# Feed-forward up projections from seven block products per pair of column tiles, and the first tap of their convolution on ScalarE

## Chip, cores, metric

The kernel runs on one core of a Trainium2 chip. The metric is the device time of one execution in microseconds (us); lower is better. TensorE is called PE here, VectorE DVE, ScalarE ACT, and SP is the engine that issues most of the DMAs.

## The reference, cut to what matters

The program is one transformer-like block with attention, a delta rule and a mixture of experts, followed by two layers (an attention mixer and an SSM mixer), each with a feed-forward. All is float32, with 512 tokens (T) and width 1024 (D). The change touches only the two feed-forwards:

```
D_FF = 2816
FFN_K = 3
...
def conv_ffn(xn, w_up, conv_w, conv_b, w_down):
    h = causal_dwconv(xn @ w_up, conv_w, conv_b)
    return (jax.nn.silu(h[..., :D_FF]) * h[..., D_FF:]) @ w_down
```

`xn @ w_up` has 2 x 2816 columns. The depthwise convolution runs along the tokens with three taps and a bias. The first 2816 columns are the gate, the others the value.

## The kernel before

Work is laid out transposed: features on the 128 partitions, tokens along the free dimension. `hT` holds the normalised input, 8 chunks (DC) of 128 features by 512 tokens. The 2816 columns are FC = 22 tiles of 128, so there are 22 pairs of a gate tile and a value tile. Weights arrive in a ring of RING = 4 slots of 1 MB, which SP refills in order: a slot is loaded again when PE has begun on the next slot (`slot_free`). One slot holds what one pair needs, 8 blocks of 128x128 for the gate tile and 8 for the value tile.

For each pair PE makes 16 matmuls of 128x512, in two accumulations of 8 (`dense`, one for each half of the pair), into two PSUM banks that alternate (`bank()`, `tile_free`, `tile_done`). ACT copies each bank to `fpad`, a buffer with two zero columns ahead of the 512 tokens. DVE does the three taps of each half: the first with the bias as one tensor_scalar (L2522), the other two as scalar_tensor_tensor (L2526). ACT then does the Silu of the gate half (L2497), and DVE multiplies both halves into `ff` (L2534). `fpad`, `fy` and `fgate` are single buffers, so the convolution of one pair ends before that of the next begins. Two pairs are written out, and the other 20 run in a hardware loop of four pairs. A small memset (L2542, `ff_ready`) then lets PE start the down projections, 22 matmuls for each of 8 output tiles; they read all of `ff`.

Each engine has one queue, written by hand, in program order. All matmuls are issued from one helper line, L391. One float32 matmul leaves two weight-load records and two matmul records in the trace, so a pair's 16 matmuls are 32 records. ffn_a is the first feed-forward and ffn_b the second; the same functions write both.

Of the kernel before, what the change touches and what calls it, by code (L numbers as in the profile page):

```python
# [405 lines left out]
def blocks(slot, first, n, width=P):  # L406
    return [slot[:, P * (first + k):P * (first + k) + width] for k in range(n)]


def program(nc, x, p, stream, vecs, consts, ssm, out):  # L410
    with ExitStack() as ctx:
# [28 lines left out]
        def V(name):  # L440
            lo, hi = VEC[name]
            return vec[:, lo:hi]
# [2010 lines left out]
        ff = a(FC, T)  # L2453
        fpad, fy = a(2, 2 + T), a(2, T)
        fgate = a(T)
        fw, fb = a(2, 3), a(2, 1)
        FF_HEAD = FC % 4

        def ffn_pe(e, before_last=None):
            def up(first=False):  # L2460
                e.eng.wait_ge(S[e.landing()], e.landed())
                w = e.slot(ring)
                for half in range(2):
                    e.eng.wait_ge(S["tile_free"], e.c["tile"].at(-1))
                    e.dense(e.bank(), blocks(w, 8 * half, 8), [hT[:, k, :] for k in range(DC)],
                            h_ready if first and half == 0 else None)
            for s in range(FF_HEAD):
                up(s == 0)
            with loop(e, FC // 4, fill=4, tile=8):
                for s in range(4):  # L2470
                    up()
            e.eng.wait_ge(S["ff_ready"], e.c["ff_ready"].next())
            for m in range(DC):
                if m == DC - 1 and before_last is not None:
                    before_last(e)
                e.eng.wait_ge(S["tile_free"], e.c["tile"].at(-1))
                o = e.bank()
                for part in range(2):
                    e.eng.wait_ge(S[e.landing()], e.landed())
                    w = e.slot(ring)  # L2480
                    for k in range(FC // 2):
                        kk = part * (FC // 2) + k
                        ins = e.mm(o, w[:, P * k:P * k + P], ff[:, kk, :], kk == 0, kk == FC - 1)
                ins.then_inc(S["tile_done"], 1)
            norm_sum_pe(e)

        def ffn_act(e, before_down=None, before_last=None):
            def up():
                e.eng.wait_ge(S["pads_free"], e.c["pads_free"].next())
                for half in range(2):  # L2490
                    e.eng.wait_ge(S["tile_done"], e.c["tile"].next())
                    t = e.result()
                    e.eng.wait_ge(S["tile_free"], e.c["tile"].at(-1))
                    nc.scalar.activation(fpad[:, half, 2:2 + T], t, ACT.Copy).then_inc(S["tile_free"], 1)  # L2494
                    e.eng.wait_ge(S["tile_free"], e.c["tile"].at())
                e.eng.wait_ge(S["gate_ready"], e.c["gate_ready"].next())
                nc.scalar.activation(fgate, fy[:, 0, :], ACT.Silu).then_inc(S["gate_silu"], 1)  # L2497
            for s in range(FF_HEAD):
                up()
            with loop(e, FC // 4, tile=8, pads_free=4, gate_ready=4):  # L2500
                for s in range(4):
                    up()
            if before_down is not None:
                before_down(e)
            residual_act(e, before_last)

        def ffn_dve(e, gain, wname, bname, meanwhile=None):
            normalize_dve(e, gain)
            fwv = V(wname).rearrange("p (j n) -> p j n", n=6)
            fbv = V(bname).rearrange("p (j n) -> p j n", n=2)  # L2510
            nc.vector.memset(fpad[:, :, 0:2], 0.0).then_inc(S["dve_chain"], 1)
            e.eng.wait_ge(S["dve_chain"], e.c["dve_chain"].next())

            def up(j):
                nc.vector.tensor_copy(fw.rearrange("p a b -> p (a b)"), dyn(fwv, j)).then_inc(S["dve_chain"], 1)
                e.eng.wait_ge(S["dve_chain"], e.c["dve_chain"].next())
                nc.vector.tensor_copy(fb.rearrange("p a b -> p (a b)"), dyn(fbv, j)).then_inc(S["pads_free"], 1)
                e.eng.wait_ge(S["pads_free"], e.c["pads_free"].next())
                for half in range(2):
                    e.eng.wait_ge(S["tile_free"], e.c["tile"].next())  # L2520
                    y = fy[:, half, :]
                    nc.vector.tensor_scalar(y, fpad[:, half, 2:2 + T], fw[:, half, 2:3], fb[:, half, :],  # L2522
                                            ALU.mult, ALU.add).then_inc(S["dve_chain"], 1)
                    e.eng.wait_ge(S["dve_chain"], e.c["dve_chain"].next())
                    for t in range(2):
                        ins = nc.vector.scalar_tensor_tensor(out=y, in0=fpad[:, half, t:t + T], scalar=fw[:, half, t:t + 1],  # L2526
                                                             in1=y, op0=ALU.mult, op1=ALU.add)
                        if (half, t) != (0, 1):
                            ins.then_inc(S["dve_chain"], 1)
                            e.eng.wait_ge(S["dve_chain"], e.c["dve_chain"].next())  # L2530
                    if half == 0:
                        ins.then_inc(S["gate_ready"], 1)
                e.eng.wait_ge(S["gate_silu"], e.c["gate_silu"].next())
                nc.vector.tensor_tensor(dyn(ff, j), fgate, fy[:, 1, :], ALU.mult).then_inc(S["dve_chain"], 1)  # L2534
                e.eng.wait_ge(S["dve_chain"], e.c["dve_chain"].next())

            for s in range(FF_HEAD):
                up(s)
            with loop(e, FC // 4, tile=8, pads_free=4, gate_silu=4, dve_chain=28) as i:
                for s in range(4):  # L2540
                    up(i * 4 + (FF_HEAD + s))
# [530 lines left out]
        @block.scalar  # L3072
        def _(act):
            e = start(Engine, "act", act)
            load_act(e)
            e.skip(2 * NB)
            e.eng.wait_ge(S["stage"], e.c["stage"].next())
            e.mark("values")
            values_act(e)
            e.eng.wait_ge(S["stage"], e.c["stage"].next())  # L3080
            e.mark("attn")
            attn_act(e)
            e.eng.wait_ge(S["stage"], e.c["stage"].next())
# [24 lines left out]
            nc.scalar.activation(dt_, V("s_dt"), ACT.Exp).then_inc(S["ssm_scalars"], 1)  # L3108
            ffn_act(e, ssm_scalars_act, ssm_turn_act)
# [5 lines left out]
            ffn_act(e)  # L3115
            e.eng.wait_ge(S["stage"], e.c["stage"].next())
            e.mark("out")
            final_act(e)

        @block.vector  # L3120
        def _(dve):
# [36 lines left out]
            ffn_dve(e, "ffn0", "f0_w", "f0_b", ssm_tables_dve)  # L3158
# [5 lines left out]
            ffn_dve(e, "ffn1", "f1_w", "f1_b")  # L3164
# [34 lines left out]
```

## Time and profile before

| | |
|---|---|
| median of 3 runs | 2922.38 us (2921.68 to 2924.26) |
| profiled execution, its own time | 2924.33 us |
| its span, first to last instruction | 2922.5 us |
| PE busy in the span | 2830.5 us (97%) |
| DVE busy | 1076.7 us (37%) |
| ACT busy | 550.9 us (19%) |
| mean granted clock of PE | 0.976 of full speed |

The span is what the trace covers. Busy time is the time in which an engine had at least one instruction under way; issuing, branches and waits are not counted.

### The profile page before, as it was taken

To read this page: it belongs to the slowest core of one execution; us is meant where nothing else is said; L and a number is where in the kernel's file an instruction comes from. 1 tells how busy PE (TensorE), PEld (TensorE's weight loads), DVE (VectorE), ACT (ScalarE), POOL (GpSimd) and SP (SyncE) were. 2 spreads that over 40 slices of the span, in tenths; PEclk is the share of its full clock that TensorE was granted. 3 is DMA by queue.
4 is the path that set the end of the run, shared out by engine and by line. 5 is a ranking of instruction groups with operands and counts; after the bars stand their busy time and mean duration, and the time that the engine had idled before them with its cause. 6 is when DMAs were issued, how large, how long until landed. Compare 5 with 4: busy or idle time off the path is not lost.

```text
span 2922.5 us, 26887 instructions
## 1 busy us (share of the span) xinstructions
PE 2830.5 (97%) x10294; PEld 1471.7 (50%) x10294; DVE 1076.7 (37%) x2357; ACT 550.9 (19%) x991; POOL 0.2 (0%) x4
## 2 busy tenths in 40 slices
PE   8999999999999999999999989999999999999998
PEld 4544446676674446444444455444444664444444
DVE  1244445556542012000033864333345663333201
ACT  2154532212301002010011143111110121111101
POOL 0000000000000000000000000000000000000000
PEclk9999989999999997999999989999999999999999
DMA  4111111101012220444412201222222211222232
GB/s 177 58 58 48 54 44 44 44 29 44 29 44 86 87 76 29 163 170 169 166 60 100 72 15 44 79 72 74 84 86 103 86 53 64 73 85 72 75 112 101
DMA packets 32936, 228.56 MB, mean 78 GB/s; under 512 B 3520, under 2 KB 4160, under 8 KB 6080
## 3 DMA queue, kind: packets, MB, share of 16 engines
q1 hardware_dynamic: 31440, 223.70, 21.5%
q10 hardware_dynamic: 1392, 3.41, 0.3%
q8 instruction: 74, 1.21, 0.2%
q14 instruction: 30, 0.25, 0.0%
HBM read 224.99 MB, written 2.10 MB: 78 GB/s over the span
## 4 chain that ended last, share of the span: by engine, by line
PE 93%; DVE 4%; ACT 2%; issue 1%; DMA 0%; DVEq 0%; ACTq 0%
PE psum L391 91%; DVE work L2316 1%; PE psum L769 1%; DVE hT L550 0%; PE psum L1078 0%; DVE work L696 0%; PE psum L2180 0%; PE psum L1879 0%; PE psum L1691 0%; PE psum L2999 0%; DVE xT L1622 0%; DMA mixT<-x_dram 0%; ACT work L521 0%; ACT work L589 0%; PE psum L612 0%
## 5 line engine op out<-in xcount | busy, mean ns | idle before, releaser
L391 PE MATMUL psum<-hT,ring 128*128 128x512 f32 (+1 forms) x3920 | 1325.0, 517 | 13.5 <-ACT work L1207 5.4
L391 PEld LDWEIGHTS psum<-hT,ring 128*128 128x128 f32 (+1 forms) x3920 | 575.6, 172 | 659.5 <-issue 645.2
L391 PE MATMUL psum<-work,ring 128*128 128x512 f32 (+1 forms) x1040 | 453.4, 597 | 16.7 <-DVE ticks L2542 8.0
L391 PEld LDWEIGHTS psum<-work,ring 128*128 128x128 f32 x1040 | 199.4, 193 | 267.0 <-issue 244.1
L391 PE MATMUL psum<-work 128*128 128x128 f32 (+7 forms) x2258 | 297.5, 286 | 14.2 <-ACT work L2278 10.9
L391 PEld LDWEIGHTS psum<-work 128*128 128x128 f32 (+2 forms) x2258 | 251.7, 178 | 109.3 <-issue 72.3
L391 PE MATMUL psum<-ring,work 128*128 (+1 forms) x568 | 248.9, 597 | 1.4 <-ACT mixT L1747 0.8
L2522 DVE TENSOR_SCALAR work<-work 128x512 f32<-128x512 f32 x88 | 48.0, 546 | 352.3 <-ACT work L2494 352.3
L391 PEld LDWEIGHTS psum<-ring,work 128*128 128x128 f32 x568 | 107.6, 192 | 132.8 <-issue 129.2
L2494 ACT ACTIVATE work<-psum 128x512 f32<-128x512 f32 x88 | 52.6, 597 | 529.4 <-PE psum L391 512.2
L391 PE MATMUL psum<-ring,hT 128*128 128x512 f32 (+2 forms) x368 | 147.6, 558 | 3.2 <-DVE work L696 1.1
L391 PE MATMUL psum<-mixT,ring 128*128 128x512 f32 x320 | 142.6, 599 | 0.7 <-ACT work L1203 0.7
L2526 DVE SCALAR_TENSOR_TENSOR work<-work 128x512 f32<-128x512 f32 x176 | 132.3, 752 | 6.2
L1622 DVE TENSOR_TENSOR xT<-xT,psum 128x512 f32<-128x512 f32 x40 | 27.5, 687 | 257.3 <-PE psum L391 257.3
L391 PEld LDWEIGHTS psum<-ring,hT 128*128 128x128 f32 x368 | 86.7, 256 | 59.6 <-issue 39.6
L521 ACT ACTIVATE work<-xT 128x512 f32<-128x512 f32 x56 | 35.2, 628 | 393.8 <-DVE xT L1622 393.1
L391 PEld LDWEIGHTS psum<-mixT,ring 128*128 128x128 f32 x320 | 61.1, 193 | 73.5 <-issue 70.9
L2316 DVE SCALAR_TENSOR_TENSOR work<-work,vec 128x512 f32<-128x512 f32 x112 | 84.1, 751 | 3.6
L1972 DVE SCALAR_TENSOR_TENSOR work<-psum,work 128x256 f32<-128x256 f32 x28 | 13.2, 483 | 188.8 <-ACT work L1954 188.3
L391 PE MATMUL psum<-work,con 128*32 128x127 f32 (+4 forms) x288 | 80.4, 463 | 2.2 <-ACT work L1349 1.1
L391 PE MATMUL psum<-con,work 128*128 128x64 f32 (+6 forms) x576 | 72.6, 253 | 8.7 <-DVE work L529 5.4
L391 PEld LDWEIGHTS psum<-con,work 128*128 128x128 f32 (+2 forms) x576 | 67.0, 175 | 15.3 <-DVE work L529 7.1
(369 smaller groups left out, 1647.6 us busy)
## 6 DMA issues: line engine op xcount, KB each, us to landing
ring<-stream_dram SPq DMA_DIRECT2D x208, 1024.0 KB, 4.8
con<-consts_dram SPq DMA_DIRECT2D x1, 2953.0 KB, 13.5
mixT<-x_dram ACTq DMA_DIRECT2D x4, 512.0 KB, 6.6
out_dram<-work SPq DMA_DIRECT2D x2, 1024.0 KB, 4.2
work<-p_dram ACTq DMA_DIRECT2D x1, 512.0 KB, 3.7
con<-ssm_dram ACTq DMA_DIRECT2D x1, 512.0 KB, 3.2
vec<-vecs_dram SPq DMA_DIRECT2D x1, 378.0 KB, 6.0
work<-consts_dram ACTq DMA_DIRECT2D x1, 256.0 KB, 2.6
```

The source lines that it names most:

```text
L391: ins = self.eng.matmul(out, lhsT, rhs, start=start, stop=stop)
L521: nc.scalar.activation(squares[:, k, :], xT[:, k, :], ACT.Square).then_inc(S["x_squares"], 1)
L769: ins = e.eng.transpose(psum[:, 2, at:at + P], a_pr[:, u.d, at:at + P], ident)
L1622: nc.vector.tensor_tensor(xT[:, m, :], xT[:, m, :], e.result(), ALU.add).then_inc(S["tile_free"], 1)
L1972: nc.vector.scalar_tensor_tensor(out=act_tok[:, s, :], in0=psum[:, gate_up_bank(ex, s), 256:512], scalar=slot_weight[:, ex, s:s + 1], in1= ...
L2316: ins = nc.vector.scalar_tensor_tensor(out=y, in0=upad[:, j, t:t + T], scalar=taps_w[:, j, t:t + 1], in1=y, op0=ALU.mult, op1=ALU.add)
L2494: nc.scalar.activation(fpad[:, half, 2:2 + T], t, ACT.Copy).then_inc(S["tile_free"], 1)
L2522: nc.vector.tensor_scalar(y, fpad[:, half, 2:2 + T], fw[:, half, 2:3], fb[:, half, :], ALU.mult, ALU.add).then_inc(S["dve_chain"], 1)
L2526: ins = nc.vector.scalar_tensor_tensor(out=y, in0=fpad[:, half, t:t + T], scalar=fw[:, half, t:t + 1], in1=y, op0=ALU.mult, op1=ALU.add)
```

## The change

The first pair is computed as before. For the 21 others (FAST) the product of weights and `hT` is cut into 2x2 blocks: rows into gate and value tile, the 1024 features into two halves of 4 chunks, and the columns into the early and the late 256 tokens. Instead of the 8 block products, 7 are made, of sums and differences of blocks (the Winograd form of Strassen's scheme). A product is 4 matmuls of 128x256, and each goes into a PSUM bank of its own (`seven`, all eight banks in turn). What comes with it:

- DVE makes four sums of `hT` blocks once for each feed-forward (`h_sums`, 128x1024 each) and four sums of weight blocks for each pair (`weight_sum`, 128x512 each, in two sets of buffers `w_sums`), reading the ring slot one pair ahead of PE.
- ACT copies product 0 out of PSUM (`base`, 128x256); DVE makes the seven additions that turn products into the four quarters of `fpad` (`read`, 128x256 each, numbered 0 to 6; `seven_read` counts them).
- ACT does the first tap and the bias (`tap0`) from `fpad` with activation Identity, where DVE's tensor_scalar was; DVE no longer copies taps and bias to small buffers. DVE keeps four taps per pair (`tap`).
- The loops over four pairs are gone; all pairs are written out. In DVE's queue the convolution of one pair (`tap`, `gated`) is mixed with the reads of the next pair and the weight sums of the pair after.

```diff
+            for j in range(FAST):
                 e.eng.wait_ge(S[e.landing()], e.landed())
                 w = e.slot(ring)
...
+                def product(i, weights, moving):
+                    for k in range(4):
+                        ins = e.mm(seven(j, i), weights[k], moving[k], k == 0, k == 3)
+                    ins.then_inc(S["seven"], 1)
+
+                if j >= 2:
+                    e.eng.wait_ge(S["seven_read"], 7 * (n + j - 1))
+                product(0, a11, b11)
+                e.eng.wait_ge(S["w_sum"], 4 * (n + j) + 3)
...
+                    e.eng.wait_ge(S["base_in"], n + j)
+                product(1, s2, t2)
...
+                product(2, s1, t1)
...
+                product(3, s3, t3)
...
+                product(4, a12, b21)
+                e.eng.wait_ge(S["w_sum"], 4 * (n + j) + 4)
...
+                product(5, s4, b22)
...
+                product(6, a22, t4)
...
+            for j in range(FC):
+                if j < FAST:
+                    e.eng.wait_ge(S["seven"], 7 * (n + j) + 1)
...
+                    nc.scalar.activation(base[:, j % 2, :], seven(j, 0), ACT.Copy).then_inc(S["base_in"], 1)
+                if j > 0:
+                    e.eng.wait_ge(S["seven_read"], 7 * (n + j))
                 for half in range(2):
...
+                    nc.scalar.activation(fy[:, half, :], fpad[:, half, 2:2 + T], ACT.Identity, scale=V(wname)[:, at:at + 1],
+                                         bias=V(bname)[:, 2 * j + half:2 * j + half + 1]).then_inc(S["tap0"], 1)
+                e.eng.wait_ge(S["gate_ready"], m + j + 1)
                 nc.scalar.activation(fgate, fy[:, 0, :], ACT.Silu).then_inc(S["gate_silu"], 1)
...
+                    read(fast, 5)
+                    read(fast, 6)
+                    e.eng.wait_ge(S["seven_read"], 7 * (n + j))
+                if j + 1 < FAST:
+                    weight_sum(j + 1, 0)
+                for t in (1, 2):
+                    for half in range(2):
+                        tap(j, half, t)
+                        if after and (half, t) == (1, 1):
+                            read(j, 0)
+                if after:
+                    e.eng.wait_ge(S["tap"], e.c["tap"].at(3))
+                    read(j, 1)
+                    read(j, 2)
+                    read(j, 3)
+                if j + 1 < FAST:
+                    weight_sum(j + 1, 2)
+                    weight_sum(j + 1, 1)
+                gated(j)
+                if j + 1 < FAST:
+                    weight_sum(j + 1, 3)
+                if after:
+                    read(j, 4)
```

PE's queue, from the second pair of ffn_a on. Before, in the loop, one pair is two rows of 8 matmuls:

```order
L2461 REGISTER_ALU
L2464 REGISTER_ALU
L391 MATMUL psum<-hT,ring 128x512 x8
L2464 REGISTER_ALU
L391 MATMUL psum<-hT,ring 128x512 x8
```

In the changed kernel one pair is these five rows (product 0; products 1 to 3, whose weights are sums in `mixT` and whose moving operands are sums in `work`; product 4; 5; 6):

```order
L391 MATMUL psum<-hT,ring 128x256 x4
L391 MATMUL psum<-work,mixT 128x256 x12
L391 MATMUL psum<-hT,ring 128x256 x4
L391 MATMUL psum<-hT,mixT 128x256 x4
L391 MATMUL psum<-work,ring 128x256 x4
```

So 16 matmuls of 512 columns became 28 of 256 columns, and the sums that 20 of them need come from DVE.

DVE's queue for the gate half of a pair in the loop before (copies of taps and bias, then three taps; the value half has three more, and L2534 multiplies the two):

```order
L2515 COPY work<-vec 128x6
L2516 ISA
L2517 ISA
L2517 COPY work<-vec 128x2
L2518 REGISTER_ALU
L2520 ISA
L2522 TENSOR_SCALAR work<-work 128x512
L2524 REGISTER_ALU
L2526 SCALAR_TENSOR_TENSOR work<-work 128x512
L2530 REGISTER_ALU
L2526 SCALAR_TENSOR_TENSOR work<-work 128x512
```

DVE's queue for one pair in the changed kernel, from the weight sum after read 6 to reads 4, 5 and 6 (L2589 are weight sums, L2614 taps, L2603 reads, L2621 the product with the gate):

```order
L2589 TENSOR_TENSOR mixT<-ring 128x512
L2614 SCALAR_TENSOR_TENSOR work<-work,vec 128x512 x2
L2603 TENSOR_TENSOR work<-work,psum 128x256
L2614 SCALAR_TENSOR_TENSOR work<-work,vec 128x512 x2
L2603 TENSOR_TENSOR work<-work,psum 128x256 x3
L2589 TENSOR_TENSOR mixT<-ring 128x512
L2589 TENSOR_TENSOR mixT<-mixT,ring 128x512
L2621 TENSOR_TENSOR work<-work 128x512
L2589 TENSOR_TENSOR mixT<-ring,mixT 128x512
L2603 TENSOR_TENSOR work<-work,psum 128x256 x3
```

Seven large operations per pair (and two small copies) became sixteen large ones: four weight sums, four taps, one product, seven reads.

## Rows read from the trace of the kernel before

**Rows 1.** The page: busy time by engine; the chain that ended last, by engine
```profile
PE 2830.5 (97%) x10294; PEld 1471.7 (50%) x10294; DVE 1076.7 (37%) x2357; ACT 550.9 (19%) x991; POOL 0.2 (0%) x4
...
PE 93%; DVE 4%; ACT 2%; issue 1%; DMA 0%; DVEq 0%; ACTq 0%
```

**Rows 2.** Windows, both up stages: us, busy by engine, PE clock, DMA share, GB/s
```profile
1853.00:2152.00 299.00, 299.00 (x698) 132.69 (x697) 109.81 (x192) 40.19 (x65) 0.00 (x0) 1.00 0.22 76
2455.00:2747.00 292.00, 292.00 (x682) 129.33 (x680) 107.80 (x190) 39.60 (x64) 0.00 (x0) 1.00 0.21 75
```

**Rows 3.** What PE waited for, 1853 to 2157 us: total, times, longest
```profile
PE psum L391 <- DVE ticks L2542: 4.0, 1, 4.0
```

**Rows 4.** Timeline of PE, runs of 512 and 128 columns: start, length, records
```profile
600.49 3.73 PE L391 MATMUL psum<-work 128*128 128x128 f32 x32
604.06 2.31 PE L391 MATMUL psum<-hT,ring 128*128 128x512 f32 x5
...
2559.56 80.85 PE L391 MATMUL psum<-hT,ring 128*128 128x512 f32 x188
```

**Rows 5.** Timeline of PE, runs of 256 columns, in the mixer
```profile
1692.25 1.13 PE L391 MATMUL psum<-work,ring 128*128 128x256 f32 x4 [0.42 <-ACT hT L2237]
...
1707.95 0.60 PE L391 MATMUL psum<-work,hT 96*128 96x256 f32 x2
1708.39 1.19 PE L391 MATMUL psum<-work 128*128 128x512 f32 x4
```

**Rows 6.** Groups by shape, PE: busy, mean ns | idle before, releasers
```profile
L391 PEld LDWEIGHTS psum<-hT,ring 128*128 128x128 f32 x2880 | 543.8, 192 | 649.4 <-issue 635.2 <-DVE ticks L366 3.7 <-PE psum L391 3.6
L391 PE MATMUL psum<-work 128*128 128x256 f32 x72 | 19.0, 382 | 0.5 <-DVE work L904 0.5
```

**Rows 7.** Groups by shape, DVE
```profile
L2526 DVE SCALAR_TENSOR_TENSOR work<-work 128x512 f32<-128x512 f32 x176 | 132.3, 752 | 6.2
L1495 DVE TENSOR_TENSOR work<-work,psum 128x512 f32<-128x512 f32 x40 | 27.6, 691 | 18.4 <-PE psum L391 18.4
L2680 DVE TENSOR_TENSOR con<-con 128x256 f32<-128x256 f32 x18 | 7.7, 427 | 0.6
```

**Rows 8.** Timeline of DVE: L2587 needs no result of L2586, L2590 needs both
```profile
2292.99 0.69 DVE L2586 TENSOR_TENSOR mixT<-mixT,con 128x512 f32<-128x512 f32 x1
2293.59 0.69 DVE L2587 TENSOR_TENSOR mixT<-mixT,con 128x512 f32<-128x512 f32 x1
2294.31 0.69 DVE L2590 TENSOR_TENSOR mixT<-mixT 128x512 f32<-128x512 f32 x1
```

**Rows 9.** Groups by shape, ACT
```profile
L2497 ACT ACTIVATE work<-work 128x512 f32<-128x512 f32 x44 | 27.7, 630 | 1.4
L1954 ACT ACTIVATE work<-psum 128x256 f32<-128x256 f32 x28 | 10.3, 382 | 165.5 <-PE psum L391 164.0 <-DVE work L1972 1.4
L2295 ACT ACTIVATE mixT<-work,vec 128x512 f32<-128x512 f32 x4 | 2.6, 710 | 0.0
```

**Rows 10.** Timeline of all engines, from the last up matmul of ffn_a on
```profile
2152.72 0.60 ACT L2494 ACTIVATE work<-psum 128x512 f32<-128x512 f32 x1 [6.27 <-PE psum L391]
...
2155.62 0.69 DVE L2534 TENSOR_TENSOR work<-work 128x512 f32 x1
2156.55 0.06 DVE L2542 MEMSET ticks<- 128x1 f32 x1 [0.24 <-DVE work L2534]
...
2156.66 23.74 PE L391 MATMUL psum<-work,ring 128*128 128x512 f32 x51 [3.98 <-DVE ticks L2542]
```

**Rows 11.** Timeline at the start of ffn_a
```profile
1848.96 31.63 PE L391 MATMUL psum<-hT,ring 128*128 128x512 f32 x69
...
1852.39 0.06 DVE L2511 MEMSET work<- 128x4 f32 x1
```

**Rows 12.** Windows, written-out code of the SSM mixer; what SP's queue waited for
```profile
2300.00:2350.00 50.00, 46.96 (x945) 38.18 (x947) 37.58 (x56) 7.96 (x14) 0.00 (x0) 0.93 0.17 54
...
SPq L3178 <- PE psum L391: 2753.6, 204, 77.0
```

More of the change, by code:

```diff
@@ new lines, in ffn_pe @@
+        def ffn_pe(e, before_last=None):
+            e.eng.wait_ge(S[e.landing()], e.landed())
+            w = e.slot(ring)
+            for half in range(2):
+                e.eng.wait_ge(S["tile_free"], e.c["tile"].at(-1))
+                e.dense(e.bank(), blocks(w, 8 * half, 8), [hT[:, k, :] for k in range(DC)], h_ready if half == 0 else None)
+            n = e.c["fast"].n
+            fill_at[n] = e.c["fill"].n
+            early, late = slice(0, HALF), slice(HALF, T)
+            for j in range(FAST):
@@ L2461, in up @@
                 e.eng.wait_ge(S[e.landing()], e.landed())
                 w = e.slot(ring)
[L2463 to L2471, printed above, removed]
+                ws = w_sums[:, j % 2, :, :]
@@ L2505, in ffn_act, with ffn_dve @@
             residual_act(e, before_last)
-        def ffn_dve(e, gain, wname, bname, meanwhile=None):
+        def ffn_dve(e, gain, wname, meanwhile=None):
             normalize_dve(e, gain)
[L2509 to L2515, printed above, removed]
-                e.eng.wait_ge(S["dve_chain"], e.c["dve_chain"].next())
[L2517 to L2541, printed above, removed]
@@ new lines, in ffn_dve @@
+            n = e.c["fast"].n
+            nc.vector.memset(fpad[:, :, 0:2], 0.0).then_inc(S["pads_free"], 1)
+            e.eng.wait_ge(S["pads_free"], e.c["pads_free"].next())
+            e.eng.wait_ge(S["h_ready"], e.c["h_ready"].at())
+            k1, k2, early, late = slice(0, 4), slice(4, 8), slice(0, HALF), slice(HALF, T)
+            for i, (o, in0, in1) in enumerate(((0, hT[:, k1, late], hT[:, k1, early]), (2, hT[:, k2, late], hT[:, k1, late]),
+                                               (1, hT[:, k2, late], h_sums[:, 0, :, :]),
+                                               (3, hT[:, k2, early], h_sums[:, 1, :, :]))):
+                if i >= 2:
+                    e.eng.wait_ge(S["h_sum"], 4 * (n // FAST) + (1, 3)[i - 2])
+                nc.vector.tensor_tensor(h_sums[:, o, :, :], in0, in1, ALU.subtract).then_inc(S["h_sum"], 1)
@@ new lines, in weight_sum @@
+            def weight_sum(j, i):
+                f = fill_at[n] + j
+                w = ring[:, f % RING, :]
+                a11, a12, a21, a22 = (w[:, 512 * q:512 * q + 512] for q in range(4))
+                ws = w_sums[:, j % 2, :, :]
+                if i == 0:
+                    e.eng.wait_ge(S["loaded%d" % (f % RING)], 16 * (f // RING + 1))
+                if j >= 2:
+                    e.eng.wait_ge(S["seven"], 7 * (n + j - 2) + 6)
+                o, in0, in1, op = ((0, a21, a22, ALU.add), (1, ws[:, 0, :], a11, ALU.subtract),
+                                   (2, a11, a21, ALU.subtract), (3, a12, ws[:, 1, :], ALU.subtract))[i]
+                if i in (1, 3):
+                    e.eng.wait_ge(S["w_sum"], 4 * (n + j) + i)
+                nc.vector.tensor_tensor(ws[:, o, :], in0, in1, op).then_inc(S["w_sum"], 1)
@@ new lines, in read @@
+            def read(j, i):
+                b = base[:, j % 2, :]
+                o, in0, product, own = ((with_low, b, 1, None), (with_add, with_low, 2, 1), (fpad[:, 1, 2 + HALF:2 + T], with_add, 3, 2),
+                                        (with_low, with_low, 3, 2), (fpad[:, 0, 2:2 + HALF], b, 4, None),
+                                        (fpad[:, 0, 2 + HALF:2 + T], with_add, 5, 3), (fpad[:, 1, 2:2 + HALF], with_low, 6, 4))[i]
+                in1 = seven(j, product)
+                e.eng.wait_ge(S["seven"], 7 * (n + j) + product + 1)
+                if i == 0:
+                    e.eng.wait_ge(S["base_in"], n + j + 1)
+                    e.eng.wait_ge(S["seven_read"], 7 * (n + j))
+                if own is not None:
+                    e.eng.wait_ge(S["seven_read"], 7 * (n + j) + own)
+                nc.vector.tensor_tensor(o, in0, in1, ALU.add).then_inc(S["seven_read"], 1)
@@ new lines, in tap @@
+            def tap(j, half, t):
+                y = fy[:, half, :]
+                at = 6 * j + 3 * half
+                wv = V(wname)[:, at:at + 3]
+                done = S["gate_ready"] if (half, t) == (0, 2) else S["tap"]
+                if t == 1:
+                    e.eng.wait_ge(S["tap0"], e.c["tap0"].next())
+                else:
+                    e.eng.wait_ge(S["tap"], e.c["tap"].at(half + 1))
+                nc.vector.scalar_tensor_tensor(out=y, in0=fpad[:, half, t - 1:t - 1 + T], scalar=wv[:, t - 1:t],
+                                               in1=y, op0=ALU.mult, op1=ALU.add).then_inc(done, 1)
@@ L2542, in ffn_dve @@
+            e.c["fast"].n += FAST
             nc.vector.memset(e.ticks, 0.0).then_inc(S["ff_ready"], 1)
```

82 lines of the change are left out of this document (61 added, 21 removed).

## The prediction

> **What bounds the kernel now.** I read the page first: PE is busy for 97% of the span and is 93% of the chain that ended last [rows 1]. Then the windows of the two up stages: PE is busy for all of the 299 and 292 us, at a granted clock of 1.00, which is the 2.4 GHz level, while DVE is busy 110 of 299 us and ACT 40 [rows 2]. Then the waits of PE over ffn_a's up stage: one, 4.0 us, at its end, for the memset behind DVE's last product [rows 3]. So the up stage is a plain stream of matmul records, and it moves with the number of records and the pace of one; the other engines cost only at its two ends.
>
> The pace is read from long runs in the timeline. 188 records of 512 columns take 80.85 us, which is 0.429 us each (the last one's length of 0.6 taken off) [rows 4]. A pair has 32 records: 13.73 us. Records of 128 columns, each with a weight load of its own, start 32 to 3.57 us (600.49 to 604.06), 0.1116 us each [rows 4].
>
> **PE, pair by pair.** A changed pair has 28 matmuls, 56 records of 256 columns. No long run of that form is in the trace, so the pace comes from both sides. On the line through the two runs it is 0.1116 + 128 x (0.429 - 0.1116)/384 = 0.2174 us. The lower end is half a 512 record, 0.2145. Two records of 256 columns in the mixer start the next work 0.44 us after the first of them, 0.22 each [rows 5]; a group of four takes 1.13 us, which is 3 x 0.2174 + 0.38, the length of one such record, and 0.10 over for the first weight load, which nothing hides after the engine has been idle [rows 5, 6]. I take 0.2174, since the line already contains a weight load and a share of waits. A pair is then 56 x 0.2174 = 12.17 us, 1.56 less than 13.73. 21 pairs in each of two feed-forwards: 42 x 1.56 = 65.4 us less. With 0.2145 it would be 72.2 less, with 0.22 59.2.
>
> The point at which nothing is gained is 13.73/56 = 0.245 us per record.
>
> Against this change speaks a rule of the Trainium skill. Rows first: a 128-column load is recorded at 192 ns in the up stage [rows 6], while 128-column matmuls with their loads follow each other every 0.1116 us [rows 4], so loads lie beside matmuls that use all rows of the array. "TensorE: Matmul & The Clock Gate", section on packing small matmuls, says that a weight load overlaps a matmul in flight only when they use different row groups. By that rule half as many columns per load would double the exposed loads. The rows above do not bear it out; what it would cost is among the rivals.
>
> **DVE, whether it keeps up.** Per pair it gets four weight sums and the product with the gate, at 0.691 each, four taps at 0.752, and seven reads at 0.427 (SBUF operands; with 512 columns a PSUM operand costs the same as none, 691 to 690) [rows 7, 8]. That is 3.46 + 3.01 + 2.99 = 9.45 us. Operations that do not need the one ahead start 0.60 apart, those that do 0.72, for a length of 0.69 [rows 8], so the queue takes between 9.45 - 16 x 0.09 = 8.0 and 9.45 + 16 x 0.03 = 9.9 us. Both are under 12.17. Before, it was 0.37 of a pair (5.0 us) [rows 2]; this engine goes from slack to about three quarters full.
>
> Order and waits matter more than the sum. Set the end of product 6 of the pair before to 0; products end every 1.74 us, at 1.7, 3.5, 5.2, 7.0, 8.7, 10.4, 12.2. DVE: read 6 to 0.5; a weight sum to 1.2. ACT stands behind product 0 (its copy comes first in its queue), copies at 1.75 to 2.15 (0.382), then does two Identity operations of 0.63 to 0.71 (Silu's length and that of an operation with a scale from `vec`) [rows 9], so the first DVE tap starts near 2.9. Two taps, read 0 (needs product 1, 3.5), two taps, read 1: to about 6.5. Reads 2 and 3 wait for product 3 at 7.0 and end at 7.8. Two weight sums to 9.0, the product with the gate (Silu ended near 6) to 9.8, the last weight sum to 10.4, reads 4 and 5 to 11.2, then a wait for product 6 at 12.2. DVE ends each round some 1.0 us early.
>
> What PE waits for in its turn: product 1 of the next pair needs the third weight sum. It is ready at 9.0 and wanted at 12.2 + 1.7 = 13.9, 4.9 us of cover. If it were gone, PE would stand in every pair. The bank waits (reads 0 to 5 of the pair before) are a whole pair old. Product 0 needs the reads of the pair before last. So the ring of waits costs nothing as long as a DVE round is under 12.17 us. Per pair ACT has 0.38 + 2 x 0.71 + 0.63 = 2.4 us, no bound.
>
> **The two ends.** At the end PE stood 3.98 us before: copy, first tap, two taps, product, memset [rows 10]. Now: read 6 (0.43), ACT's first tap (0.63 to 0.71), three DVE taps started 0.65 apart and the fourth, Silu of the gate half beside it, the product 0.69, and the same 0.35 from its end to PE (2155.62 + 0.69 to 2156.66) [rows 7, 9, 10]. The taps start at 1.2; the gate's second ends at 1.2 + 1.3 + 0.75 = 3.25, Silu at 3.95, the product at 4.7, PE at 5.05. That is 1.1 us later, twice: +2.1 us. At the start the four `hT` sums (twice the length of a 512-column operation at most, 1.38) and the first four weight sums are 8.3 us on DVE from 1852.4, so to 1860.8 [rows 7, 11]; the first pair keeps PE until at least 1848.96 + 13.73 = 1862.7 [rows 11], and product 0 for 1.7 more. Cost nothing; without that cover it would be 8.3 us per feed-forward.
>
> **Edits at nothing.** The code is written out instead of looped, over 9 PE instructions per us; the SSM mixer's written-out part runs 945 matmuls and 947 loads in 50 us, 38 per us [rows 12]. Its supply can hold this. Ring: a slot is used every 12.2 instead of 13.7 us, SP waits for PE 2753.6 us in all, not for DMA, and the DMA share of the stage is 0.22 [rows 2, 12]. DVE's small copies and first tap lay under PE before; their removal gives nothing by itself.
>
> **Sum.** -65.4 + 2.1 = -63.3 us. The profiled execution had 2924.33 us, 1.8 above its span; it becomes 2861.0. It lies 1.95 above the median of the runs shown, so the median becomes 2859.1. With the low pace: 2922.4 - 72.2 + 2 = 2852; with 0.22: 2865.
>
> **Rivals.**
> 1. *Each product pays for its wait.* All seven products start behind a wait of their own. For: after idle time the first load costs 0.10 us [rows 5]. Against: the loop before had waits and register work every 16 records and kept 0.429, and loads lie beside matmuls there. If all seven paid it: 7 x 0.10 x 42 = 29 us, time 2888. A third of it gives 2869.
> 2. *The weight load is not hidden under 256 columns* (slower). Its place is every record of the 42 pairs. For: nothing in the trace is a long run of 256 columns, and records of 512 hide a load of 192 ns easily, records of 256 only just. Against: the 0.1116 of 128 columns and the 0.22 of 256 [rows 4, 5]. If each record paid the 0.10 of a first load, a pair is 56 x 0.317 = 17.75 us, +4.02 x 42 = +169, with the ends 3093. It decides from 0.245 us per record, 0.028 above mine.
>  By the row-group rule of the Trainium skill (same page and section), with the page's own load time of columns/1.2 ns, an estimate is 0.107 us more per record, much the same in time, and a quarter of this rival's chance is its; the trace disagrees.
> 3. *DVE becomes the bound.* For: sixteen large operations and a queue in fixed order. Against: 9.9 us at the most by rows. It would need 0.15 us more at each of the sixteen to reach PE's 12.17, and 0.24 to reach 13.73, from where it is slower. At a round of 13.0 it is 42 x 0.73 less, 2894; at 15 it is 42 x 1.27 more, 2978.
>
> **How the numbers follow.** The main case has 0.80, with 2850 to 2868 as its own range (paces 0.2145 to 0.22, the ends, and a part of the waits). Rival 1 in the rest of its reach, 2868 to 2890, has 0.11. Rival 2 has 0.04, rival 3 0.04 (half of it above 2922), and 0.01 goes to no change. The range 2848 to 2880 holds the main case and most of rival 1. About 0.2%, 6 us, is what a measurement of this kernel can tell: faster 0.93, same 0.01, slower 0.06.
>
> **What would show it.** The window of an up stage with PE busy all through at clock 1.00 and 0.217 us per record; an up stage of 13.7 + 21 x 12.2 = 269 us instead of 302; DVE busy about 75% there, each round ending in a wait for PE; the wait for the memset at 5.0 us. Wrong would be: waits of PE for DVE's weight sums or reads inside the stage, idle "issue" in PE between products, a granted clock under 1.00, table loads on ACT between Identity and Silu, or DVE operations well longer than those of rows 7.

## The result

| | before | changed |
|---|---|---|
| median | 2923.32 us (2921.68 to 2924.57, 4 runs) | 2852.48 us (2851.28 to 2859.27, 4 runs) |
| ratio of the runs | | 0.9769 (0.9756 to 0.9782) |
| profiled execution, its span | 2922.5 us | 2849.5 us |

The change is faster by 2.3%. A second set, 4 runs of the changed kernel beside 25 further runs of the kernel before (median 2918.60 us), gave 0.9770 (0.9753 to 0.9788). All ratios below are to such runs of the kernel before, taken beside the kernel in question; each has its 95% interval behind it. The predicted 2859 us is a ratio of 0.978.

The page of the changed kernel, busy time by engine:

```profile
PE 2753.9 (97%) x11302; PEld 1658.9 (58%) x11302; DVE 1226.2 (43%) x2651; ACT 578.4 (20%) x1037; POOL 0.2 (0%) x4
```

PE lost 77 us of busy time and is still busy for 97% of a shorter span [rows 1]. DVE gained 150 us; of these only what stands at the two ends of the stages shows in the time, 1.1 us each, as the rows below tell.

Windows inside the two up stages of the changed kernel (us, busy by engine, PE clock, DMA share, GB/s):

```profile
1860.00:2105.00 245.00, 245.00 (x1137) 215.68 (x1136) 172.59 (x325) 48.41 (x81) 0.00 (x0) 1.00 0.25 86
2430.00:2670.00 240.00, 240.00 (x1113) 211.28 (x1112) 168.69 (x317) 48.35 (x80) 0.00 (x0) 1.00 0.26 88
```

PE is busy all the time at the full clock, as before [rows 2], and DVE for 70% in place of 37%. What PE waited for in the whole program, the row of the memset behind the last product (L2656 is L2542 of before):

```profile
PE psum L391 <- DVE ticks L2656: 10.3, 2, 5.1
```

5.1 us twice, where it was 4.0 [rows 3]. Between the first and the last product of a stage the timeline of PE shows no wait at all.

One round in the timeline of the changed kernel, PE, DVE and ACT together:

```profile
1962.63 1.89 PE L391 MATMUL psum<-hT,ring 128*128 128x256 f32 x8
1962.83 0.42 DVE L2603 TENSOR_TENSOR work<-work,psum 128x256 f32<-128x256 f32 x1 [1.24 <-PE psum L391]
1963.28 0.69 DVE L2589 TENSOR_TENSOR mixT<-ring 128x512 f32<-128x512 f32 x1
...
1964.36 5.34 PE L391 MATMUL psum<-work,mixT 128*128 128x256 f32 x24
1964.56 0.38 ACT L2547 ACTIVATE work<-psum 128x256 f32<-128x256 f32 x1 [7.86 <-PE psum L391]
1964.84 1.51 ACT L2552 ACTIVATE work<-work,vec 128x512 f32<-128x512 f32 x2
1965.67 1.46 DVE L2614 SCALAR_TENSOR_TENSOR work<-work,vec 128x512 f32<-128x512 f32 x2 [1.70 <-ACT work L2552]
...
1968.82 0.42 DVE L2603 TENSOR_TENSOR work<-work,psum 128x256 f32<-128x256 f32 x1
1969.54 1.89 PE L391 MATMUL psum<-hT,ring 128*128 128x256 f32 x8
1969.73 0.75 DVE L2603 TENSOR_TENSOR work<-work,psum 128x256 f32<-128x256 f32 x2 [0.50 <-PE psum L391]
...
1974.92 0.42 DVE L2603 TENSOR_TENSOR work<-work,psum 128x256 f32<-128x256 f32 x1 [1.24 <-PE psum L391]
...
1976.44 5.34 PE L391 MATMUL psum<-work,mixT 128*128 128x256 f32 x24
```

The reader is to see two things. The row of products 1 to 3 starts again after 12.08 us (1964.36 to 1976.44), and PE's rows carry no idle time in brackets. Over ten rounds it is 12.09 us (1855.58 to 1976.44), 0.2158 us for each of 56 records. And DVE, from read 6 to read 6 (1962.83 to 1974.92), stands three times: 1.70 us for ACT's first tap, 0.50 for product 3, 1.24 for product 6. That is 3.44 us in 12.09, so DVE's own work is 8.65.

The end of ffn_a's up stage, which answers to [rows 10]:

```profile
2107.87 0.42 DVE L2603 TENSOR_TENSOR work<-work,psum 128x256 f32<-128x256 f32 x1 [1.31 <-PE psum L391]
2108.32 1.52 ACT L2552 ACTIVATE work<-work,vec 128x512 f32<-128x512 f32 x2 [6.56 <-DVE work L2603]
2109.24 2.74 DVE L2614 SCALAR_TENSOR_TENSOR work<-work,vec 128x512 f32<-128x512 f32 x4 [0.95 <-ACT work L2552]
2111.35 0.63 ACT L2555 ACTIVATE work<-work 128x512 f32<-128x512 f32 x1 [1.51 <-DVE work L2614]
...
2112.08 0.69 DVE L2621 TENSOR_TENSOR work<-work 128x512 f32<-128x512 f32 x1
...
2112.84 0.06 DVE L2656 MEMSET ticks<- 128x1 f32 x1
...
2112.96 67.53 PE L391 MATMUL psum<-work,ring 128*128 128x512 f32 x150 [5.13 <-DVE ticks L2656]
```

Read 6, two first taps on ACT, four taps on DVE, Silu, the product, the memset: a chain with PE standing.

### The profile page after: what moved, and what is told of

Its sections match the earlier page's. It is cut to its first block, busy times and chain, and to the rows that moved or that the text cites. A ratio compares the mean times of both kernels' runs of the same rounds, so it can differ in the third digit from the quotient of the medians.

```text
span 2849.5 us, 28832 instructions
## 1 busy us (share of the span) xinstructions
PE 2753.9 (97%) x11302; PEld 1658.9 (58%) x11302; DVE 1226.2 (43%) x2651; ACT 578.4 (20%) x1037; POOL 0.2 (0%) x4
## 4 chain that ended last, share of the span: by engine, by line
PE 93%; DVE 4%; ACT 2%; issue 1%; DMA 0%; DVEq 0%; ACTq 0%
PE psum L391 91%; DVE work L2316 1%; PE psum L769 1%; DVE hT L550 0%; PE psum L1078 0%; DVE work L696 0%; PE psum L2180 0%; PE psum L1879 0%; PE psum L3113 0%; DVE xT L1622 0%; ACT work L521 0%; ACT work L589 0%; DVE work L2614 0%; DMA mixT<-x_dram 0%; ACT mixT L1729 0%
## 5 line engine op out<-in xcount | busy, mean ns | idle before, releaser
L391 PE MATMUL psum<-hT,ring 128*128 128x512 f32 (+2 forms) x3248 | 905.2, 458 | 13.8 <-ACT work L1207 5.5
L391 PEld LDWEIGHTS psum<-hT,ring 128*128 128x128 f32 (+1 forms) x3248 | 447.2, 168 | 355.1 <-issue 323.8
L391 PE MATMUL psum<-work,ring 128*128 128x512 f32 (+1 forms) x1376 | 532.5, 543 | 18.9 <-DVE ticks L2656 10.3
L391 PEld LDWEIGHTS psum<-work,ring 128*128 128x128 f32 x1376 | 262.8, 192 | 277.3 <-issue 244.3
L391 PE MATMUL psum<-work,mixT 128*128 128x256 f32 (+2 forms) x1200 | 258.6, 379 | 2.0 <-ACT work L1732 1.5
L391 PEld LDWEIGHTS psum<-work,mixT 128*128 128x128 f32 (+1 forms) x1200 | 207.1, 181 | 44.7 <-issue 16.1
L2614 DVE SCALAR_TENSOR_TENSOR work<-work,vec 128x512 f32<-128x512 f32 x176 | 125.6, 748 | 74.4 <-ACT work L2552 74.4
L2603 DVE TENSOR_TENSOR work<-work,psum 128x256 f32<-128x256 f32 x294 | 115.8, 417 | 77.5 <-PE psum L391 76.1
L2316 DVE SCALAR_TENSOR_TENSOR work<-work,vec 128x512 f32<-128x512 f32 x112 | 84.1, 751 | 3.6
L2547 ACT ACTIVATE work<-psum 128x256 f32<-128x256 f32 x42 | 16.1, 384 | 316.5 <-PE psum L391 316.5
```

The costliest lines, as they stand in the source:

```text
L391: ins = self.eng.matmul(out, lhsT, rhs, start=start, stop=stop)
L2316: ins = nc.vector.scalar_tensor_tensor(out=y, in0=upad[:, j, t:t + T], scalar=taps_w[:, j, t:t + 1], in1=y, op0=ALU.mult, op1=ALU.add)
L2547: nc.scalar.activation(base[:, j % 2, :], seven(j, 0), ACT.Copy).then_inc(S["base_in"], 1)
L2603: nc.vector.tensor_tensor(o, in0, in1, ALU.add).then_inc(S["seven_read"], 1)
L2614: nc.vector.scalar_tensor_tensor(out=y, in0=fpad[:, half, t - 1:t - 1 + T], scalar=wv[:, t - 1:t], in1=y, op0=ALU.mult, op1=ALU.add).then_ ...
```

## Experiments

**Two more traces.** Both kernels were run again unchanged, because the two first traces differ by 73 us while the predicted sum was 63: some 10 us lay ahead of ffn_a, in code that the change does not touch.

> The kernel before, unchanged, for a second trace of it. In the two traces so far the part of the program ahead of ffn_a, which the change does not touch, ends 10.2 us apart: the first hT operation of ffn_a (L550) starts at 1847.1 us before and at 1836.9 us after. Theory 1 (those 10 us are chance of the clock dips and no part of the change): over the runs this start moves by several us either way, in this kernel too. Theory 2 (the longer written-out code shifts something in the unchanged part for good): it is again 1847 within 2 us here, and 1837 in every kernel with the written-out code. Time 2923 by both.

> The changed kernel, unchanged, for a second trace and a second ratio. Theory 1: L550 of ffn_a starts anywhere from 1837 to 1848, the part behind it takes 1012.6 us again, the median lies between 2851 and 2860. Theory 2: 1837 within 2 us again, and a median of 2852.

Measured: 2919.44 us (ratio 0.9997, 0.9985 to 1.0009) and 2854.21 us (0.9770, 0.9753 to 0.9788). The first `hT` operation of ffn_a stands at 1847.1 us in the first trace of before (5.3 us ahead of the memset in [rows 11]). In the timeline of the changed kernel:

```profile
1836.89 5.36 DVE L550 SCALAR_TENSOR_TENSOR hT<-xT,vec,psum 128x512 f32<-128x512 f32 x8 [1.83 <-PE psum L391]
```

In the second trace of before:

```profile
1840.07 5.35 DVE L550 SCALAR_TENSOR_TENSOR hT<-xT,vec,psum 128x512 f32<-128x512 f32 x8 [2.17 <-PE psum L391]
```

And in the second of the changed kernel:

```profile
1840.79 5.36 DVE L550 SCALAR_TENSOR_TENSOR hT<-xT,vec,psum 128x512 f32<-128x512 f32 x8 [1.81 <-PE psum L391]
```

The looped kernel was 7 us earlier in its second trace, the written-out one 4 us later. Over all traces of this study the start lies at 1840.1 to 1847.1 in the five looped kernels and at 1836.9 to 1843.3 in the seven written out. The idea that it stays at 1847 in the one and at 1837 in the other falls. What moves it is not shown. What is behind that point took 1075.4 and 1078.3 us before (span less start), and 1012.6 and 1012.6 after: 63 to 66 us less.

That stretch still holds code that the change does not touch: the down projections, the SSM mixer and the program's end. To take them out, the two up stages are measured alone, each up to the first down matmul. PE's rows at the start of ffn_b's up stage and of its down projections, before:

```profile
2443.22 304.05 PE L391 MATMUL psum<-hT,ring 128*128 128x512 f32 x704 [0.93 <-DVE hT L550]
2751.25 109.22 PE L391 MATMUL psum<-work,ring 128*128 128x512 f32 x247 [3.98 <-DVE ticks L2542]
```

And in the changed kernel:

```profile
2403.24 18.53 PE L391 MATMUL psum<-hT,ring 128*128 128x512 f32 x40 [0.93 <-DVE hT L550]
2678.99 121.49 PE L391 MATMUL psum<-work,ring 128*128 128x512 f32 x279 [5.12 <-DVE ticks L2656]
```

ffn_b, from its first up matmul to its first down matmul, takes 308.0 us before and 275.8 after. ffn_a, from its first `hT` operation to its first down matmul, takes 309.6 (1847.1 to 2156.66 [rows 10]) and 276.1 (1836.89 to 2112.96). Both stages together are 617.6 and 618.1 us in the two traces of before, and 551.8 in both of the changed kernel: 65.8 to 66.3 us less. The stretch between the two stages, from the first down matmul of ffn_a to the first up matmul of ffn_b, is unchanged code; it took 286.6 and 289.6 before and 290.3 and 290.3 after.

**The form of the records alone.**

```diff
-                    e.dense(e.bank(), blocks(w, 8 * half, 8), [hT[:, k, :] for k in range(DC)],
...
+                    o = e.bank()
...
+                    for cols in (slice(0, T // 2), slice(T // 2, T)):
+                        for k in range(DC):
+                            ins = e.mm(o[:, cols], blocks(w, 8 * half, 8)[k], hT[:, k, cols], k == 0, k == DC - 1)
+                    ins.then_inc(S["tile_done"], 1)
```

The first pair of each stage stays as it was, and so does the loop over four pairs.

> The kernel before with each 128x512 matmul of 21 pairs (all but the first two pairs' first) of the up stage cut into two of 128x256 into the same bank: 64 records of 256 columns per pair in place of 32 of 512, all 8 block products, no sums. Theory 1 (pace of a record is its columns and 2.5 ns, weight loads hidden): 64 x 0.2158 = 13.81 us per pair in place of 13.73, +0.08 x 42 = +3.5 us, 2927. Rival (the pace of 0.2158 depends on few loads per stretch or on the sums' short groups, a load shows under longer runs): more than 13.9 us per pair, over 2930. The difference to the changed kernel, which keeps the form of the records and drops one product in eight, is then what the seventh of the products is worth: 8 x 0.2158 x 42 = 72.5 us.

Measured: 2923.44 us, ratio 1.0009 (0.9998 to 1.0021). Its timeline in the up stage, PE:

```profile
1869.66 90.60 PE L391 MATMUL psum<-hT,ring 128*128 128x256 f32 x419
```

(90.60 - 0.38)/418 = 0.2158 us, the same as in the changed kernel, with twice as many weight loads per column as before. Its two up stages, measured as above, take 621.4 us against 617.6 and 618.1, so 3.3 to 3.8 more where 3.5 were expected. All that the cut into 256 columns costs is the fixed part of a record; the gain is the product that is left out. This kernel has the loop and the changed one has not, and both run at 0.2158, so writing the pairs out gave PE nothing either.

**The first tap on ACT alone**, in the kernel before:

```diff
+                    nc.scalar.activation(fy[:, half, :], fpad[:, half, 2:2 + T], ACT.Identity, scale=fw[:, half, 2:3],
+                                         bias=fb[:, half, :]).then_inc(S["tap0"], 1)
...
-                    nc.vector.tensor_scalar(y, fpad[:, half, 2:2 + T], fw[:, half, 2:3], fb[:, half, :],
-                                            ALU.mult, ALU.add).then_inc(S["dve_chain"], 1)
-                    e.eng.wait_ge(S["dve_chain"], e.c["dve_chain"].next())
+                    e.eng.wait_ge(S["tap0"], e.c["tap0"].next())
```

> The kernel before with only the second part of the change: the first tap and bias of each half done by ACT behind its copy, in place of DVE's operation; the taps still come from the small copies. Theory 1 (PE sets the up stage, this lies under it): no change in the stage, and at each of the two ends 0.80 us (ACT's length in the changed kernel) in place of 0.55, so +0.5 us: 2923 to 2924. Rival (moving it off DVE was itself a gain): under 2918.

Measured: 2920.30 us beside 2918.60 of before, ratio 1.0000 (0.9989 to 1.0012), where +0.5 us or nothing was expected; the interval is 3 us to each side. PE's waits at the two ends went from 8.0 to 8.5 us in all, as expected.

**The first tap back on DVE**, in the changed kernel:

```diff
-                    nc.scalar.activation(fy[:, half, :], fpad[:, half, 2:2 + T], ACT.Identity, scale=V(wname)[:, at:at + 1],
-                                         bias=V(bname)[:, 2 * j + half:2 * j + half + 1]).then_inc(S["tap0"], 1)
...
+                    nc.vector.tensor_scalar(fy[:, half, :], fpad[:, half, 2:2 + T], V(wname)[:, at:at + 1],
+                                            V(bname)[:, 2 * j + half:2 * j + half + 1], ALU.mult, ALU.add).then_inc(S["tap0"], 1)
```

> The changed kernel with the first tap and its bias back on DVE (one tensor_scalar of 0.55 us for each half, ahead of the other taps); everything else stays. Theory 1 (PE sets the stage as long as DVE's round is under 12.09 us): DVE has 3.4 us of waits per round and gets 1.1 more work, of which the wait for ACT's tap (1.7 us) goes away, so the stage stays at 12.09 per pair. At the ends DVE's first tap stands in place of ACT's 0.80, but both halves lie on DVE: +0.3 us each. Within 1 us of the changed kernel, 2852 to 2856. Rival (the two parts of the change need each other, DVE would become the bound): 42 x 0.5 us or more, over 2873.

Measured: 2854.58 us, ratio 0.9771 (0.9756 to 0.9786); the changed kernel's 0.9769 and 0.9770 lie within that interval. PE's wait at each end is 5.2 us. The window of its up stage:

```profile
1870.00:2105.00 235.00, 235.00 (x1091) 206.87 (x1090) 183.50 (x350) 20.04 (x40) 0.00 (x0) 1.00 0.26 90
```

DVE is busy for 78% and PE still for all of it. The second half of the change is worth nothing that these runs can tell, with the seven products or without them, where a difference under some 4 us would not show.

**How much room DVE has.** Three, six and nine more additions of 128x512 per pair:

```diff
+                for s in range(9):
+                    if s >= 2:
+                        e.eng.wait_ge(S["spare"], e.c["spare"].at(-1))
+                    nc.vector.tensor_tensor(spare[:, s % 2, :], xT[:, 0, :], xT[:, 1, :], ALU.add).then_inc(S["spare"], 1)
+                    e.c["spare"].n += 1
                 gated(j)
```

> The changed kernel with nine more DVE additions of 128x512 per pair into a spare buffer, between the weight sums and the product with the gate. They are extra work and change no result. Each takes 0.60 us of DVE's queue. Theory 1 (DVE's round is 8.65 us of work and 3.4 us of waits that all can give way): 8.65 + 5.4 = 14.1 us, a little more for ACT's first tap, so 2.0 to 2.3 us over PE's 12.09 for 42 pairs and 5.4 at each end: +95 to +107 us, 2950 to 2962. Rival (waits in fixed order do not give way, each addition costs its full time): 5.4 x 44 = +238 us, 3092. Rival (DVE has more room than that): under 2920.

> The changed kernel with three more DVE additions of 128x512 per pair into a spare buffer, at the same place as the nine. Theory 1: 1.8 us more in a round with 3.4 us of waits; the stage stays at 12.09 us per pair. The wait before read 6 (1.24) goes and read 6 comes 0.6 us later; the wait for ACT's tap takes that up. Only at the end of each stage it shows, 1.8 us behind the taps, of which Silu (0.7) covers a part, and 0.6 ahead of them: +3 to +5 us in all, 2856 to 2859. Rival (every addition to DVE shows, as the nine did with 5.4 us of work against 2.2 us of time per pair): +26 us or more.

> The same with six more. Theory 1: the round with nine measured 14.25 us, three fewer are 1.8 less, 12.45, just over PE's 12.09: 0.3 to 0.4 us per pair, +13 to +17 in the stages and 3 to 7 at the ends, 2869 to 2878. This is the threshold: with fewer, DVE's work is free, from here on each costs its 0.60. Rival as for three: +100 us.

| additions | time | ratio (95%) | DVE's round | PE's round | PE's wait at each end |
|---|---|---|---|---|---|
| 0 (two sets) | 2852.48, 2854.21 us | 0.9769, 0.9770 | 12.09 us | 12.09 us | 5.1 us |
| 3 | 2854.41 us | 0.9777 (0.9760 to 0.9795) | 12.09 us | 12.09 us | 6.7 us |
| 6 | 2876.11 us | 0.9847 (0.9830 to 0.9863) | 12.44 us | 12.09, then 12.44 us | 14.0 us |
| 9 (2 runs) | 2955.06 us | 1.0116 (1.0096 to 1.0137) | 14.25 us | 12.09, then 14.25 us | 19.2 us |

The timeline of the kernel with nine, one round:

```profile
1967.85 0.69 DVE L2590 TENSOR_TENSOR mixT<-mixT,ring 128x512 f32<-128x512 f32 x1
1968.45 5.50 DVE L2654 TENSOR_TENSOR work<-xT 128x512 f32<-128x512 f32 x9
1968.59 5.45 PE L391 MATMUL psum<-work,mixT 128*128 128x256 f32 x24 [1.66 <-DVE mixT L2590]
1973.87 0.68 DVE L2622 TENSOR_TENSOR work<-work 128x512 f32<-128x512 f32 x1
...
1982.70 5.50 DVE L2654 TENSOR_TENSOR work<-xT 128x512 f32<-128x512 f32 x9
```

Here DVE is the bound, and PE stands 1.66 us of each round for the third weight sum, the wait that the prediction named as the first to fail. The other 0.5 us of the 2.16 that a round got longer lie in PE's rows beside its waits; products 1 to 3, for one, take 5.45 us behind the stand where they took 5.34. 1.8 us of DVE's work left the round at 12.09, 5.4 made it 2.16 longer, and from six to nine each addition costs 0.60 us of the round. With nine the kernel is slower than before.

The table has a second reading. With six, DVE's round is 12.44 us from the start, but PE does not follow it until late. PE's row of products 1 to 3 in that kernel:

```profile
2015.51 5.34 PE L391 MATMUL psum<-work,mixT 128*128 128x256 f32 x24
...
2027.59 5.34 PE L391 MATMUL psum<-work,mixT 128*128 128x256 f32 x24
...
2039.92 5.45 PE L391 MATMUL psum<-work,mixT 128*128 128x256 f32 x24
...
2052.36 5.45 PE L391 MATMUL psum<-work,mixT 128*128 128x256 f32 x24
```

For 14 rounds, from 1858.38 to 2027.59, PE keeps 12.09 us; then it takes 12.33 and 12.44. That is what the cover of 4.9 us for the third weight sum, worked out in the prediction, allows: DVE falls back 0.35 us per round, and 14 x 0.35 is 4.9. With nine the cover lasts three rounds. What DVE has fallen back by is paid at the end of the stage, where PE waits for DVE's last product, and with it the additions of the last pair: 4.9 + 6 x 0.60 = 8.5 us would be this estimate for six, and the wait grew by 8.9. For nine it would be 10.3 and the wait grew by 14.1, so not all of that is accounted for. From the first up matmul of ffn_a to the last, PE took 270.0 us in the changed kernel and 272.2 with six additions; the wait behind it went from 5.1 to 14.0. So of the 22 us that six additions cost in the two stages, 18 are at the ends and only 4 in the rounds. With nine the ends have 28 us of 101. The expectations for six and nine put 3 to 7 and 11 us there and more into the rounds; that their times came out (2869 to 2878 and 2950 to 2962 us) is in part two errors that cancel. With three the time was a little under the 2856 to 2859 expected; the two waits at the ends grew by 3.2 us in all, within its 3 to 5.

**Down projections that don't wait for the last tile.** PE stands 5.1 us twice for the last of 22 tiles, which it reads only in its 22nd matmul.

```diff
-            e.eng.wait_ge(S["ff_ready"], e.c["ff_ready"].next())
+            e.eng.wait_ge(S["ff_part"], e.c["ff_part"].next())
...
                         kk = part * (FC // 2) + k
+                        if m == 0 and kk == FC - 1:
+                            e.eng.wait_ge(S["ff_ready"], e.c["ff_ready"].next())
...
                 gated(j)
+                if j == FC - 2:
+                    nc.vector.memset(e.ticks, 0.0).then_inc(S["ff_part"], 1)
```

In the kernel before, the same is done with a small memset behind the product of every pair, so it has 22 memsets more per feed-forward.

> The changed kernel, but PE may begin the down projections when 21 of the 22 tiles of ff are there (a memset behind the product of tile 20 lets it), and waits for the last tile only ahead of the 22nd matmul of the first output tile, some 18 us of matmuls later. Theory 1 (the 5.1 us stand at each end is the whole cost of the tail, and the records behind it run slow for a few us): the two waits of 5.1 us go, and with them part of the slow records, 10 to 17 us less: 2836 to 2844 at a level of 2853. Rival (the time of the tail comes back as a wait at the 22nd matmul or at the next bank): less than 3 us.

> The kernel before with the same early start of the down projections (a small memset per pair counts the tiles of ff). Theory 1: its two waits of 4.0 us go, 8 us and part of the slow records behind them, 8 to 14 us less, so a ratio of 0.995 to 0.997. It is then the fair partner for the changed kernel with the early start: the difference of the two is 42 x 1.64 = 69 us, without the 2.3 us of longer tails. Rival as above: ratio 0.999 or more.

Measured: 2837.08 us, ratio 0.9719 (0.9705 to 0.9732), and 2909.31 us, ratio 0.9954 (0.9937 to 0.9971), both as expected. Neither trace has a wait of PE at the end of an up stage. The windows behind the stage's end, in the changed kernel:

```profile
2113.00:2123.00 10.00, 10.00 (x17) 4.37 (x18) 7.48 (x35) 3.59 (x7) 0.00 (x0) 0.71 0.29 107
2123.00:2133.00 10.00, 10.00 (x24) 4.38 (x24) 0.00 (x0) 0.00 (x0) 0.00 (x0) 1.00 0.29 105
```

Behind the end of ffn_b's up stage:

```profile
2679.00:2689.00 10.00, 10.00 (x20) 4.54 (x21) 0.00 (x0) 0.52 (x2) 0.00 (x0) 0.85 0.31 105
```

In the one with the early start, behind ffn_a:

```profile
2118.00:2128.00 10.00, 10.00 (x25) 4.50 (x24) 8.02 (x38) 4.17 (x7) 0.00 (x0) 1.00 0.37 132
```

After the stand of 5.1 us PE had a granted clock of 0.71 on the mean of 10 us, so part of them at the 1.2 GHz level, and started 17 records where 24 fit. Without the stand the clock is 1.00. So in ffn_a the stand cost about 7 x 0.43 = 3 us more behind it, 8.1 in all. In ffn_b it was 5.1 + 4 x 0.43 = 6.8. Together that is 15 us, which is how far the ratios 0.9719 and 0.9770 are apart. The traces are further apart, 992.0 us behind the start of ffn_a against 1012.6; the other 5 us lie for the most part in the unchanged stretch between the stages, and their cause is not shown. This is the fastest version of the study. The two kernels with the early start differ by 0.9719/0.9954 = 0.976, 69 us (72 between their medians), so the gain of the seven products stands with either way of ending the stage.

## Why the prediction was right

**The bound.** It named a plain stream of records, and both stages of the changed kernel are one: PE busy at a clock of 1.00 in every window behind the first pair, no wait. The up stage of ffn_a ran from 1837.8 to 2107.8 us, 270.0 us. Predicted were 269, and that it came so close is in part luck: the 21 changed pairs took 253.8 us in place of 255.6, and the first pair about 16.1 in place of 13.7, at a granted clock of 0.86 (window 1837.8 to 1854). The sum has no term for that slow start. Before, the stage took 304.7 us where the prediction has 302, with a clock of 0.85 in its first 16 us, so it drops out of the difference.

**The pace.** Predicted 0.2174 us per record, measured 0.2158. The term "65.4" was mis-sized: 42 x (13.73 - 12.09) = 68.9 us. The line between 128 and 512 columns was too high by 1.6 ns, since its lower end, the 128-column run at 0.1116, carries more per record than the long runs do; why was not tested. A record of 512 at 0.429 and one of 256 at 0.2158 fit 0.833 ns per column and about 2.5 ns on top. "TensorE: Matmul & The Clock Gate" of the Trainium skill gives columns/2.4 + 2.5 ns at the 2.4 GHz level for a matmul by itself, in its section on the back-to-back issue gap; a float32 record here takes twice the columns' time and the 2.5 ns once.

**The weight loads (rival 2).** The loads lie under matmuls of 256 columns fully: 419 records in a row at 0.2158 in the split kernel, each with a load, which is recorded at 191 ns in that kernel, on all rows of the array. The row-group rule of the Trainium skill that was weighed does not hold here. Rival 1, a gap at each product's wait, fell too: the run of 24 records with two waits inside takes 5.34 us, (5.34 - 0.38)/23 = 0.2157 each. Its 0.10 for a first load after idle time was right in size, where PE did stand: 5.45 for 5.34 in the kernel with nine additions.

**DVE.** The bounds of 8.0 and 9.9 us hold the measured 8.65. The schedule was right to some tenths: a wait of 1.24 before read 6 where 1.0 was said, and the wait for product 3 (0.50 for 0.5), and for ACT's tap. Rival 3 did not come about. Its bounds hold: it was to cost something from a round of 12.17 us and to be slower from 13.73, and the kernels with rounds of 12.44 and 14.25 lie on the two sides of the kernel before. Its prices do not: they count 42 longer rounds and nothing at the ends, and the runs showed fewer longer rounds and longer waits at the ends.

**The ends.** Predicted 5.05 us, measured 5.13; the chain of operations was the one described. ACT's first tap was mis-sized: 0.803 us with scale and bias from `vec`, not 0.63 to 0.71. Two operations start 0.71 apart, so the last DVE tap is still not late for it. At the start the sums took 7.4 us in place of 8.3 (1842.2 to 1849.6) and PE wanted them at 1855.6; they cost nothing, as predicted. The table load between Identity and Silu that the prediction lists as a sign of being wrong stands once in each stage, in the first pair, as it does before, and PE doesn't wait for it. The cost of the stand behind its own end, the records at the slow clock, was left out of the sum. It was there before as well: over the 10 us behind the stands of 4.0 us the clock was 0.86 in ffn_a and 0.69 in ffn_b, against 0.71 and 0.85 behind those of 5.1 us. The 308 down matmul records of ffn_a took 134.0 and 135.3 us in the two traces before and 135.3 in both after, so in ffn_a at most 1.3 us of it is new.

**The sum.** -63.3 predicted. The two up stages with their ends say -65.8 to -66.3, and the measured terms give -68.9 + 2.3 = -66.6, so they account for the stages within 1 us. Against the prediction the pace gave 3.5 us more and the ends took 0.2 more. Behind the point where the change begins the traces say -62.8 (1012.6 against 1075.4) and -65.7; the medians of the first set say -70.8, its interval -64 to -71, and the second set -67 (ratio 0.977 of 2919). What these differ by from the stages is within what unchanged code moves by itself, 10 us from trace to trace ahead of ffn_a and up to 4 between the stages; why it moves is not shown.

## What to carry to other kernels

Where one engine streams without a wait, count its records and find the pace of the new form from runs on both sides of it; that put a change of 2.3% within 0.3% of the time. Work on another engine leaves the round as it is up to the point where that engine's own round, waits taken out, is as long as the bound's: list its waits in one round, since their sum is the room (3.4 us of 12.1 here). Past that point it does not show in the rounds at once but eats the cover of the operand that is wanted first, and then shows; and what it has fallen back by is paid at the end of the stage, so look there too. A stage that ends in a stand is worth a look in itself: letting the next stage begin without its last operand gave 15 us for a few lines.

## What the hardware showed that was not expected

- ACT's Identity from SBUF with a scale and a bias read from `vec` takes 803 ns for 128x512, where a Silu without them takes 630. "ScalarE: Activation LUTs" of the Trainium skill, in its section on what a table load costs, gives 186 + 0.833 ns per element and about 93 ns for each operand of one value per partition. An estimate by it is 799 ns for this one; the trace agrees.
- A stand of 1.66 us of PE in every round of 14.25 left its granted clock at 1.00 over a window of 250 us, while one of 5.1 us was followed by 0.71 over 10 us. How long the stand was made no difference beyond 4 us: the 308 down records behind it took 134.0 to 135.3 us after stands of 4.0 us, 135.3 after 5.1, 134.5 after 6.7, 135.0 after 14.0 and 134.9 after 19.2.
- Unchanged code in front of the change reached the same point at 1836.9 to 1847.1 us in 12 traces, with no difference in its source.

The window of the kernel with nine additions for the second point:

```profile
1875.00:2125.00 250.00, 223.73 (x1001) 187.07 (x999) 243.13 (x440) 45.60 (x72) 0.00 (x0) 1.00 0.22 76
```
